# Differential attention: slopes in the queries, scores two tiles ahead, an order for each engine

## The reference

```python
def block(args):
    q_blk, i = args
    t = i * Q_BLOCK + jnp.arange(Q_BLOCK)
    s = jnp.einsum('bqhcd,bkhcd->bhcqk', q_blk, k)          # q was scaled by 64 ** -0.5
    dist = jnp.abs(t[:, None] - pos[None, :])
    bias = -slopes[:, None, None] * dist
    allowed = (pos[None, :] // CHUNK) <= (t[:, None] // CHUNK)
    s = jnp.where(allowed, s + bias[None, :, None], -jnp.inf)
    p = jax.nn.softmax(s, axis=-1)
    attn = p[:, :, 0] - lam * p[:, :, 1]
    return jnp.einsum('bhqk,bkhe->bqhe', attn, v)
```

## Time and profile before

| | us |
|---|---|
| median of 3 runs | 2958.15 (2957.37 to 2966.26) |
| profiled execution, its own time | 2959.86 |
| its span | 2958.6 |
| the attention stage in it | 2563.1 to 2830.1 |

### The profile page before, as it was taken

The page is one execution under the profiler, slowest core; times in us unless marked ns, Lnnn a source line. Parts: engine busy times, 40 slices in busy tenths (PEclk is TensorE's granted clock), DMA queues, the critical chain, the costliest instruction groups (busy, mean ns, idle before and its releaser), DMA issues.

```text
span 2958.6 us, 49843 instructions
## 1 busy us (share of the span) xinstructions
PE 2739.6 (93%) x20906; PEld 2198.7 (74%) x20906; DVE 1410.7 (48%) x2610; ACT 954.2 (32%) x1930; POOL 603.3 (20%) x532
## 2 busy tenths in 40 slices
PE   7999979999999999989999997888879999999969
PEld 5776668788888888778778864878757878766647
DVE  4426664333333333452455306777654333377753
ACT  4215753311111111242122122444453122255452
POOL 2214243211111111134211101222113102122111
PEclk9999999999999999999999996999989999999989
DMA  3211031111111111111211210010023201111032
GB/s 101 54 57 43 30 136 57 36 57 43 57 47 46 50 50 43 57 57 55 81 36 36 68 59 1 4 32 4 4 93 114 79 15 52 33 33 35 28 117 114
DMA packets 152479, 156.66 MB, mean 53 GB/s; under 512 B 4920, under 2 KB 124346, under 8 KB 150722
## 3 DMA queue, kind: packets, MB, share of 16 engines
q1 hardware_dynamic: 152258, 153.47, 16.1%
HBM read 131.40 MB, written 22.05 MB: 52 GB/s over the span
## 4 chain that ended last, share of the span: by engine, by line
PE 81%; DVE 7%; POOL 3%; ACT 3%; issue 3%; DMA 2%; SPq 0%; DVEq 0%; ACTq 0%; POOLq 0%
PE ps L888 14%; PE ps L890 13%; PE ps L889 13%; PE ps L2359 7%; PE ps L943 5%; PE ps L945 5%; PE ps L944 5%; PE ps L1764 3%; PE ps L1509 2%; PE ps L1511 2%; PE ps L1510 2%; PE ps L1841 2%; PE ps L1855 1%; DVE r L853 1%; PE ps L1872 1%
## 5 line engine op out<-in xcount | busy, mean ns | idle before, releaser
L888 PE MATMUL ps<-r,r 128*128 128x512 f32 (+1 forms) x1760 | 699.9, 398 | 9.1 <-DVE r L853 5.1
L890 PE MATMUL ps<-r,r 128*128 128x512 f32 (+1 forms) x1760 | 685.5, 390 | 0.0
L889 PE MATMUL ps<-r,r 128*128 128x512 f32 (+1 forms) x1760 | 685.3, 389 | 0.0
L834 POOL TENSOR_TENSOR sb<-sb 128x1024 f32<-128x1024 f32 x134 | 269.8, 2023 | 1230.6 <-DMA sb<-in_w_ffn_up 484.2
L888 PEld LDWEIGHTS ps<-r,r 128*128 128x128 f32 x1760 | 333.3, 189 | 101.2 <-issue 24.1
L853 DVE TENSOR_TENSOR r<-sb,r 128x1024 fp32r<-128x1024 f32 x182 | 240.3, 1336 | 315.4 <-ACT r L848 315.1
L890 PEld LDWEIGHTS ps<-r,r 128*128 128x128 f32 x1760 | 332.9, 189 | 69.4
L889 PEld LDWEIGHTS ps<-r,r 128*128 128x128 f32 x1760 | 333.4, 189 | 65.6 <-issue 1.5
L943 PE MATMUL ps<-r,r 128*128 128x512 f32 (+1 forms) x768 | 303.6, 395 | 55.4 <-ACT r L1431 27.8
L2359 PE MATMUL ps<-sb 64*64 64x64 f16 (+2 forms) x8832 | 268.5, 216 | 32.2 <-issue 11.5
L945 PE MATMUL ps<-r,r 128*128 128x512 f32 (+1 forms) x768 | 294.7, 384 | 0.0
(11 more groups left out here) (257 smaller groups left out, 3424.3 us busy)
## 6 DMA issues: line engine op xcount, KB each, us to landing
sb<-in_a_w_in SPq DMA_DIRECT2D x29, 512.0 KB, 4.0
sb<-in_w_out SPq DMA_DIRECT2D x24, 512.0 KB, 6.5
sb<-in_w_ffn_gate SPq DMA_DIRECT2D x22, 512.0 KB, 4.0
sb<-in_w_ffn_up SPq DMA_DIRECT2D x22, 512.0 KB, 4.0
sb<-in_w_ffn_down SPq DMA_DIRECT2D x22, 512.0 KB, 3.5
sb<-in_w_in SPq DMA_DIRECT2D x17, 512.0 KB, 4.0
xs<-sb SPq DMA_DIRECT2D x4, 2048.0 KB, 6.9
gates<-sb SPq DMA_DIRECT2D x32, 256.0 KB, 2.0
```

Source lines behind the costliest of these rows:

```text
L834: pool.tensor_tensor(w.raw, w.raw, w.gain.unsqueeze(2).broadcast_to((P, w.nk, w.n)), ALU.mult).then_inc(*s.w_gain.up(w.id))
L888: pe.matmul(self.out, w.hi[:, q, self.cols], hi, start=(q == 0), stop=False)
L889: pe.matmul(self.out, w.hi[:, q, self.cols], lo, start=False, stop=False)
L890: ins = pe.matmul(self.out, w.lo[:, q, self.cols], hi, start=False, stop=(q == w.nk - 1))
```

## The change

The slope moves from the bias strip into the queries and the exponential: queries are copied with 0.125/slope(i), the strip stays plain distances, and the exponential and the negated maximum take slope(i) as scale. The strip's scalings go. The tiles' work is laid out by an order for each engine, `ORDER_DIFF`: scores and bias run two tiles ahead of the transposes, the exponentials one. Values are split in two steps: `Turned`, all the transposes of a tile and their copies, and `Valued`, all its products with the values. A tile's gate units lie in one run, between them. The second half's buffer is reused once its tile is combined, in place of once it is transposed.

```diff
-        dve.tensor_scalar(self.dst(st.i)[:, st.span], st.out, self.scale, None, ALU.mult)
+        dve.tensor_scalar(self.dst(st.i)[:, st.span], st.out, self.scale(st.i), None, ALU.mult)
...
+    ORDER_DIFF = {
+        "pe": "U:0 C:2 G:0 W:0 T:-1",
+        "dve": "N:0 A:-1 M1:2 M0:2 G:0",
+        "act": "X1:1 U:0 X0:1 T:-1 G:0",
+        "pool": "G:0",
+        "sp": "G:0",
+    }
+
+    def steps_diff(self, parts):
+
+        last = self.n * ST - 1
+        kinds = {"C": (Scores,), "M0": (Biased, (0,)), "M1": (Biased, (1,)), "X0": (Exponentials, (0,)), "X1": (Exponentials, (1,)), "N": (Normalise,),
+                 "U": (Turned,), "W": (Valued,), "A": (ScaleOut,), "T": (TurnOut,)}
+        made, out = {}, []
+        for t in range(-2, last + 2):
+            for engine, names in self.ORDER_DIFF.items():
+                for name, ahead in (word.split(":") for word in names.split()):
+                    at = t + int(ahead)
+                    if name == "G":
+                        out += [Alone(self.k, step, engine) for step in parts.get(at, ())]
+                        continue
+                    if not 0 <= at <= last:
+                        continue
+                    if (name, at) not in made:
+                        kind, *more = kinds[name]
+                        made[name, at] = kind(self.k, self, *divmod(at, ST), *more)
+                    out.append(Alone(self.k, made[name, at], engine))
+        return out
...
@@ class Alone
+        if engine == "pe":
+            self.weights, self.paces = step.weights, step.paces
...
@@ class Biased
-                dve.wait_ge(*s.turned_p.at((of.id, of.last_group(*was, h))))
+                dve.wait_ge(*(s.combined.at((of.id, *was, 0)) if of.diff and h else s.turned_p.at((of.id, of.last_group(*was, h)))))
...
-            dve.tensor_scalar(s4[:, 1:2], s4[:, 0:1], -1.0, None, ALU.mult)
+            dve.tensor_scalar(s4[:, 1:2], s4[:, 0:1], -of.scale(i), None, ALU.mult)
...
-            act.activation(sc, sc, ACT.Exp, bias=s4[:, 1:2], accum_out=s4[:, 2:3])
+            act.activation(sc, sc, ACT.Exp, bias=s4[:, 1:2], scale=of.scale(i), accum_out=s4[:, 2:3])
...
+class Turned(Values):
+    def __init__(self, k, of, i, iq):
+        AttentionStep.__init__(self, k, of, i, iq)
+        self.turned, self.valued = of.groups(i, iq), []
+
+class Valued(AttentionStep):
+    def pe(self, pe):
+        k, s, of, i, iq = self.k, self.s, self.of, self.i, self.iq
+        nj, b = of.nkeys(iq) // P, of.out_bank(iq)
+        k.bank_free(pe, b)
+        for g, h, first, m in of.groups(i, iq):
+            pe.wait_ge(*s[of.copied(g)].at((of.id, g)))
+            for j in range(m):
+                ins = pe.matmul(k.ps[:, b, 0:P], of.pt[g % 2][:, j * P:(j + 1) * P], of.v(i, first + j),
+                                start=(first + j == 0), stop=(first + j == nj - 1))
+            ins.then_inc(*s.valued.up((of.id, g)))
...
     def dve_pair(self, dve, att, i):
-        dve.tensor_scalar(self.strip, self.strip, slope(i) / (slope(i - 1) if i else 1.0), None, ALU.mult)
+        pass
...
-    ev_q = EvictNormed(k, lambda i: q[:, i, :], 0.125)
+    ev_q = EvictNormed(k, lambda i: q[:, i, :], lambda i: 0.125 / slope(i))
...
-    yield from [Ring(k, k.ring[:2]), *att.steps(between(k, prods)), Join(k), fetch, Ring(k, k.ring)]
+    yield from [Ring(k, k.ring[:2]), *att.steps_diff(between(k, prods)), Join(k), fetch, Ring(k, k.ring)]
...
@@ def between(k, prods)
+    parts = {}
     for t in range(BT * ST):
+        n = by_tile[t // ST >= 4][t % ST]
+        group, units = units[:n], units[n:]
+        for st, of_st in itertools.groupby(group, key=lambda unit: unit[0]):
+            part = Part(k, st, [q for _, q in of_st], act_later=True)
+            parts.setdefault(t, []).append(part)
+            if part.last:
+                parts.setdefault(t + 1, []).append(Gated(k, st))
```

More of the change, by code:

```diff
@@ L1090, in dve @@
         dve.wait_ge(*s.linear.at(st.id))
-        dve.tensor_scalar(self.dst(st.i)[:, st.span], st.out, self.scale, None, ALU.mult).then_inc(*s.copied_dve.up(st.id))
+        dve.tensor_scalar(self.dst(st.i)[:, st.span], st.out, self.scale(st.i), None, ALU.mult).then_inc(*s.copied_dve.up(st.id))
 class EvictTokens(Evict):
@@ L1597, in __init__ @@
         self.sc = k.at(sc, 4, S)
+        self.scale = slope if diff else lambda i: 1.0
         self.pt = [k.at(at, HALF) for at in pt]
@@ L1609, in buf @@
         return (2 * iq + h) % 4
[L1611 to L1633, removed]
     ORDER = {
@@ L1718, in __init__, with plan @@
         self.step, self.engine = step, engine
+        if engine == "pe":
+            self.weights, self.paces = step.weights, step.paces
+    def plan(self):
+        if self.engine == "pe":
+            self.step.plan()
     def sp(self, sp):
@@ L1790, in dve @@
             dve.wait_ge(*s.biased.at((of.id, i, iq, h)))
-            dve.tensor_scalar(s4[:, 1:2], s4[:, 0:1], -1.0, None, ALU.mult).then_inc(*s.maxed.up((of.id, i, iq, h)))
+            dve.tensor_scalar(s4[:, 1:2], s4[:, 0:1], -of.scale(i), None, ALU.mult).then_inc(*s.maxed.up((of.id, i, iq, h)))
 class Exponentials(AttentionStep):
@@ L1804, in act @@
             act.wait_ge(*s.maxed.at((of.id, i, iq, h)))
-            act.activation(sc, sc, ACT.Exp, bias=s4[:, 1:2], accum_out=s4[:, 2:3]).then_inc(*s.exped.up((of.id, i, iq, h)))
+            act.activation(sc, sc, ACT.Exp, bias=s4[:, 1:2], scale=of.scale(i), accum_out=s4[:, 2:3]).then_inc(*s.exped.up((of.id, i, iq, h)))
 class Normalise(AttentionStep):
@@ L1844, in pe @@
         if self.valued:
-            (self.values if of.diff else self.values_across)(pe)
+            self.values(pe)
     def values(self, pe):
[L1848 to L1860, removed]
         k, s, of, i, iq = self.k, self.s, self.of, self.i, self.iq
@@ L1893, in dve @@
                 dve.tensor_copy(of.pt[g % len(of.pt)][:, 0:m * P], k.ps[:, 4 + g % 2, 0:m * P]).then_inc(*s.pt_dve.up((of.id, g)))
+class Turned(Values):
[13 more added lines that the diff above has]
+            ins.then_inc(*s.valued.up((of.id, g)))
+        k.free[b] = ("scaled_out", (of.id, i, iq))
 class ScaleOut(AttentionStep):
@@ L2033, in dve_pair @@
     def dve_pair(self, dve, att, i):
[L2034 to L2037, removed]
+        pass
     def bias(self, att, i, iq, h):
-        return self.strip[:, S - (iq + 1) * P:S], ("strip", i)
+        return self.strip[:, S - (iq + 1) * P:S], ("step_dve", "dist_masked")
 def slope(j):
@@ L3158, in layer_a @@
     z = EvictShift(k, lambda j: lora if j == 18 else (r, key, v)[j // BT][:, j % BT, :], zt, dz, V["a_shift_mu_2"])
-    ev_m = EvictNormed(k, lambda i: q_mem[:, i, :], -0.125)
+    ev_m = EvictNormed(k, lambda i: q_mem[:, i, :], lambda i: -0.125)
     jobs = [(j * P, z, j) for j in range(12, 16)] + [(mem0 + j * P, ev_m, j) for j in range(2)]
@@ L3251, in layer_b @@
     k.product_banks = 2
-    ev_k = EvictNormed(k, lambda i: key[:, i, :])
-    ev_m = EvictNormed(k, lambda i: q_mem[:, i, :], -0.125)
+    ev_k = EvictNormed(k, lambda i: key[:, i, :], lambda i: 1.0)
+    ev_m = EvictNormed(k, lambda i: q_mem[:, i, :], lambda i: -0.125)
     jobs = [(w_kv, i * P, kvn, ev_k, i) for i in range(4)] + [(w_in, 2 * BR + i * P, pre, ev_m, i) for i in range(2)]
@@ L3301, in between @@
     by_tile = ([4, 4, 4, 4, 3, 3, 2, 0], [4, 4, 3, 3, 2, 0, 0, 0])
-    places = {0: [], 1: [2], 2: [1, 2], 3: [0, 1, 2], 4: [0, 1, 2, 2]}
-    table, left = {}, 0
+    parts = {}
     for t in range(BT * ST):
-        for place in places[by_tile[t // ST >= 4][t % ST]]:
-            if units:
-                table.setdefault((t, place), []).append(units.pop(0))
-    assert not units
[L3310 to L3320, removed]
+        n = by_tile[t // ST >= 4][t % ST]
[5 more added lines that the diff above has]
+                parts.setdefault(t + 1, []).append(Gated(k, st))
+    assert not units
+    return parts
 def with_weights(k, steps):
```

## The result

The changed kernel takes 3022.1 us (median of 4 runs, 3018.3 to 3028.0); its ratio to the kernel before is 1.0211, with a 95% interval of 1.019 to 1.0231. A later comparison on another chip gave 1.0201 (1.0183 to 1.022). It is slower, as forecast, but by some 63 us where 44 were forecast: 2 us above 3020, the upper end of the stated range (and 4 above the 3018 of case 1 alone).

A forecast was written before the change was run, and what follows sets the result against it. Waits between TensorE and VectorE were to bound the differential attention: 278.0 us of slots, 23.4 of roundings and 10 of clock falls made 311.4 against 267.0, 44.4 more; 3002.6 us against the median, range 2972 to 3020.

The forecast's parts named there:

- case 1: The sum as forecast, a slower kernel: 3002.6 us, its own range 2985 to 3018; chance 0.70.
- The ring: In differential attention, normalise, transposes, scores and bias-and-maximum wait in a closed circle; slots summed to 278.0 us, 11.0 more.
- The copy of the product: VectorE's copy of a finished gate product, 0.71 us with its gap, stands ahead of the next slot's normalise.
- The rounding: Weights' cast on ACT and subtraction on VectorE stand ahead of normalise, leaving TensorE empty before seven tiles: 23.4 us.
- the clock's: TensorE's granted clock falls to 0.50 after idle of some 2.5 us; about nine falls, 1.1 us each: 10 us.
- 2 (roundings hidden): Roundings cost nothing and the clock falls no more often than before: +16.5 us, 2975; chance 0.11.
- 4 (faster): VectorE's rest ends before TensorE's in every slot, so the stage is TensorE's stream: about 2936 us; chance 0.07.
- Case 3: TensorE's clock falls in every second slot, 24 falls, 26 us in place of 10: 3018.6 us; chance 0.09.
- the arithmetic part: Slopes in the query's copy and scales in the exponential and negated maximum add no instruction and cost nothing.

The follow-up runs named there:

- e4: Changed kernel with TensorE doing the scores of the tile after next ahead of the transposes; ratio 1.0038 to the kernel before.
- e9: Changed kernel with the product's copy behind the next normalise and the weights' rounding behind the maxima, scores left behind the transposes; ratio 1.0049 to the kernel before.
- e5: Changed kernel with scores ahead of the transposes, product's copy behind the next normalise and rounding behind the maxima; ratio 0.9952 to the kernel before.
- e2: Changed kernel with VectorE's copy of a finished gate product moved behind the next slot's normalise; ratio 1.0153 to the kernel before.
- e3: Changed kernel with the weights' rounding moved: cast ahead of ACT's output copy, subtraction behind VectorE's second maximum; ratio 1.0099 to the kernel before.
- e11: Changed kernel repeated without alteration, beside the others on one chip; ratio 1.0201 to the kernel before.
- e1: Kernel before, old order kept, with slopes in the queries' copy and exponentials' scale and without the six strip scalings; ratio 0.9992 to the kernel before.
- e10: Kernel before with POOL's two operations on a gate tile cut from 512 columns to 1; ratio 0.9994 to the kernel before.
- e6: Changed kernel with POOL's two operations on a gate tile cut from 512 columns to 1; ratio 1.0165 to the kernel before.

## Why the prediction was right, and where it was not

**The ring** was right. Counted from the first transpose of a tile to that of the next, at full clock and without a rounding, the slots came out as summed: tile 1's 6.23 us (6.15 given), tile 2's 5.38 (5.4), tile 3's 7.13 (7.1), tile 4's 6.60 (6.6), tile 5's 7.33 (7.3), tile 6's 5.55 (5.4), tile 7's 3.86 (3.9). Four slots stand out. Tile 5's in the last two pairs took 10.59 us where 7.3 was given: 1.4 of it is scores at half clock, and 1.6 to 2.0 VectorE's factor and combination beside POOL. Tile 0's in pairs 2 and 4 took 5.71 where 4.3 was given, at full clock, with the combination at 2.08 in place of 0.48. e4 opens the ring and e9 against e5 has it alone; both show what it costs.

**The copy of the product**: 1.1 to 1.3 us each was given; moving it took 14.2 us of idle from 16 places (e2), 0.9 each. The wait was right, its size a little high.

**The rounding**: 23.4 us was given. The slots that hold one took 8.65 us (tile 7; 3.9+4.1 given), 9.91 (tile 3; 7.1+3.1), 8.60 (tile 1; 6.15+2.6), counted the same way. e3 took 16.9 us of idle away and left the subtraction's own time in the slot. Right.

**TensorE's idle time in sum**: the forecast stage at full clock, 278.0+23.4 = 301.4, less TensorE's work there (244.45 less half of 17.1, 235.9) is 65.5 us. Measured: 67.1.

**The step that failed is the clock's**: "I expect about nine falls, at the seven roundings and after tile 5 in the last two pairs: 10 us". The reason was right, the size was not. At 1.1 us a fall it put 10 us where the 51.2 us at half clock cost half of that, 25.6: 15.6 of the 16.5 us by which the profiled stage, 327.9, is longer than the 311.4 forecast. (The median missed by 19.5; the profiled execution is 3.8 us under the median.) Both its factors were too small:

- The number. Each stretch at 0.50 lasted 3.4 or 6.8 us; counted in 3.4 us there were five before and 15 after. Of the 15, two stand at the stage's start, eight at six of the seven roundings (two of them with 6.8 us), and five in the last two pairs, at the gaps before tiles 37, 38, 45 and 46, where one a pair was forecast. In the repeat e11 all seven roundings have one. In e3 the time at half clock goes back to 17.1 us, so the roundings' gaps brought most of what is new; e4 shows that they bring fewer where the ring is open.
- The price. A stretch of 3.4 us costs 1.7 us of TensorE's work. My 1.1 compared a pair with a fall to one without and so counted only what the gap did not take back: TensorE's busy time differs by 1.43 between those two rows.

One profile does not fix this term: e1, as fast as the kernel before and with the same 22.0 us of idle in the same places, had 27.3 us at half clock in its profiled execution against 17.1.

**What was left out**, put at nothing without a reason: the meetings of VectorE and POOL. Two traces of it stood in the kernel before (the strip's scaling took 0.68 to 1.50 us and L853 1.22 to 1.76; in e10 they take 0.68 and 1.22), and the change moved the gates' tanh to the end of ACT's slot, so POOL's work fell on VectorE's normalise, now on the path. It is worth 11 to 14 us by e6's ratio and 8.6 in its profiled stage. It did not show in the sum: without it, idle is 60.9 (e6), so my 65.5 was some 5 us too high elsewhere, and the two errors met. That idle time came out within 2 us of the forecast is in part luck. The Trainium skill ("GPSIMD Engine Reference", Specifications) says that POOL shares its SBUF interfaces with VectorE, and that VectorE's instructions with two SBUF inputs or in a 2-port perf mode contend with it; for two inputs the rows agree (the factor and the combination are stretched to 1.12 and 2.24 us, and the maxima, whose other input is in PSUM, are not: 1.22 us at 1024 columns in both kernels), and it should have been in the sum.

**Rivals**: 2 (roundings hidden) and 4 (faster) are out by e3, e2 and e4. Case 3 came nearest, 3018.6, and by luck: its clock term of 26 us is what was measured, but it is 24 falls of 1.1 us in every second slot, and there were 15 stretches of 1.7, most of them behind long gaps; e3's 17 short gaps at full clock are against its reason. That the arithmetic part costs nothing is shown by e1.

## What to carry to other kernels

When scores run ahead on TensorE, put them ahead of the transposes that wait for VectorE; look for a ring by following each engine's queue once round, not only the data. A step that is inserted by its place in a list moves on every queue when the list is regrouped by engine; find it again on each. Price a long gap on TensorE with the half-speed stretch that may follow it, and ask of each VectorE operation that comes onto the path whether POOL is working at that time.

## What the runs showed of the hardware that was not expected

- A gap of under 2 us was followed by a fall. Here TensorE waited 1.95 us (0.29 and 0.48 in the two slots before), the granted clock went from 1.00 to 0.50 some 0.5 us after its return to work, and the scores behind it took 3.40 us (1.92 stands for the same width in the earlier trace rows):

```profile
2814.13 1.11 PE L1853 MATMUL ps<-sb 128*128 128x128 f32 x6 [1.95 <-DVE sb L1834]
...
2815.16 3.40 PE L1776 MATMUL ps<-sb 64*128 64x512 f32 x8
```

```profile
2815.00:2815.50 0.50, 0.50 (x4) 0.50 0.00 0
```

Yet in the kernel before the gap of 2.52 us stands four times, and a fall comes at two of them; in e1 the same four gaps have one each.

- A VectorE instruction of one column took up to 1.12 us instead of 0.22 beside POOL, and a combination of 256 columns 2.08 us instead of 0.48 where it met POOL's gain of 1.90:

```profile
2785.02 1.90 POOL L834 TENSOR_TENSOR sb<-sb 128x1024 f32<-128x1024 f32 x1
...
2785.12 2.08 DVE L1834 SCALAR_TENSOR_TENSOR sb<-sb 128x256 f32<-128x256 f32 x1
```

- TensorE's busy time in the stage less half of its time at half clock is 230.5 to 239.2 us in the profiles of all the kernels here, for the same work, so what the clock costs can be read off the granted clock to some 4 us.
